# The turning steps of a chunked recurrence: products with the unit matrix in place of a mix of transpositions and products

## The reference

```
def step(state, inp):
    r_t, w_t, k_t, v_t, a_t, b_t = inp
    sa = jnp.einsum('bhvk,bhk->bhv', state, a_t)
    state = state * w_t[:, :, None, :] + sa[..., None] * b_t[:, :, None, :] \
            + v_t[..., None] * k_t[:, :, None, :]
    return state, jnp.einsum('bhvk,bhk->bhv', state, r_t)
s0 = jnp.zeros((B, H, N, N), jnp.float32)
_, ys = lax.scan(step, s0, xs)
```

## Time and profile before

| | |
|---|---|
| median of 3 runs | 2541.79 us (2538.91 to 2542.49) |
| the profiled execution | 2542.76 us, its span 2541.0 us |
| TensorE busy | 2371.4 us, 93% |
| GpSimd, VectorE, ScalarE busy | 1217.3, 1062.3 and 680.2 us |
| mean granted clock of TensorE | 0.961 |
| rchunks | from 1090.29 to 1311.8 us |

### The profile page before, as it was taken

One profiled execution on the slowest core, in us unless ns is written; L12 is line 12 of the kernel. 1 busy time (PEld: TensorE's weight loads), 2 busy tenths in 40 slices (PEclk: granted clock), 3 DMA queues, 4 the chain that ended last, 5 costly groups with the idle time before them and its releaser, 6 DMA issues.

```text
span 2541.0 us, 39706 instructions
## 1 busy us (share of the span) xinstructions
PE 2371.4 (93%) x15724; PEld 1730.5 (68%) x15724; DVE 1062.3 (42%) x1674; ACT 680.2 (27%) x1255; POOL 1217.3 (48%) x690
## 2 busy tenths in 40 slices
PE   4999998899999799989989967998999999899999
PEld 1445776688878444479966645666887787688877
DVE  5975852555500346643341344663224431422200
ACT  2125112333300234423323113672002231333300
POOL 1007885588876000000025401557877325688876
PEclk8999999999999799989989985998999999999999
DMA  7630532222222112200002140001323231232222
GB/s 278 233 105 26 220 128 67 66 99 99 91 91 97 44 62 70 66 13 4 4 11 73 60 157 1 2 2 58 100 92 107 88 103 58 75 99 95 95 91 99
DMA packets 59336, 211.63 MB, mean 83 GB/s; under 512 B 6720, under 2 KB 7752, under 8 KB 59200
## 3 DMA queue, kind: packets, MB, share of 16 engines
q1 hardware_dynamic: 48816, 175.61, 20.6%
q0 software_dynamic: 6432, 22.45, 2.5%
q10 hardware_dynamic: 3952, 11.58, 1.2%
HBM read 207.45 MB, written 8.45 MB: 85 GB/s over the span
## 4 chain that ended last, share of the span: by engine, by line
PE 64%; POOL 18%; issue 11%; DVE 4%; ACT 1%; DMA 1%; POOLq 0%; ACTq 0%; DVEq 0%; SPq 0%
PE banks L368 14%; POOL WH L404 9%; PE banks L424 9%; PE banks L425 9%; PE banks L426 9%; POOL WL_A L407 8%; PE banks L1473 3%; PE banks L1428 2%; PE banks L561 2%; PE banks L574 2%; PE banks L593 2%; DMA W<-stream 1%; PE banks L1508 1%; PE banks L1506 1%; PE banks L1926 1%
## 5 line engine op out<-in xcount | busy, mean ns | idle before, releaser
L404 POOL TENSOR_TENSOR WH<-W,ZERO 128x1024 fp32r<-128x1024 f32 x240 | 467.4, 1947 | 681.9 <-PE banks L426 371.5
L407 POOL TENSOR_TENSOR WL_A<-W,WH 128x1024 fp32r<-128x1024 f32 x164 | 419.9, 2560 | 12.9
L368 PE MATMUL banks<-H,W 128*128 128x512 f32 x752 | 332.7, 602 | 20.1 <-ACT H L735 15.1
L424 PE MATMUL banks<-HF,WH 128*128 128x512 f32 x704 | 276.6, 393 | 14.7 <-DVE HF L516 7.7
L368 PEld LDWEIGHTS banks<-H,W 128*128 128x128 f32 x752 | 144.3, 193 | 207.2 <-issue 204.1
L425 PE MATMUL banks<-HF,WH 128*128 128x512 f32 x704 | 275.7, 392 | 0.0
L426 PE MATMUL banks<-HF,WL_A 128*128 128x512 f32 x704 | 275.4, 391 | 0.0
L425 PE MATMUL banks<-HR,WH 128*128 128x512 f32 x416 | 168.3, 404 | 0.0
L424 PEld LDWEIGHTS banks<-HF,WH 128*128 128x128 f32 x704 | 132.9, 189 | 47.3 <-issue 15.7
L426 PEld LDWEIGHTS banks<-HF,WL_A 128*128 128x128 f32 x704 | 133.3, 189 | 27.7
L425 PEld LDWEIGHTS banks<-HF,WH 128*128 128x128 f32 x704 | 133.3, 189 | 26.9
(11 more groups left out here) (414 smaller groups left out, 4591.6 us busy)
## 6 DMA issues: line engine op xcount, KB each, us to landing
W<-stream SPq DMA_DIRECT2D x328, 512.0 KB, 3.5
BIG<-stream ACTq DMA_DIRECT2D x20, 512.0 KB, 6.3
BIG<-stream POOLq DMA_DIRECT2D x12, 512.0 KB, 6.8
bias_rows<-bias_lines POOLq DMA_DIRECT2D x1, 4096.0 KB, 21.9
BIG<-bias_rows POOLq DMA_DIRECT2D x1, 4096.0 KB, 16.9
X<-x_t POOLq DMA_DIRECT2D x1, 2048.0 KB, 16.4
bias_rows<-bias_lines POOLq DMA_DIRECT2D x1, 2048.0 KB, 18.8
BIG<-bias_rows POOLq DMA_DIRECT2D x1, 2048.0 KB, 11.0
```

Source lines behind the costliest of these rows:

```text
L368: last = nc.tensor.matmul(bank, W[:, slot, (lo + k) * P:(lo + k + 1) * P], r, start=(k == 0), stop=(k == len(rhs) - 1))
L404: nc.gpsimd.tensor_tensor(WH[:, half, :], W[:, slot, :], ZERO[:, 0:1].to_broadcast([P, D]), ALU.add)\
L407: nc.gpsimd.tensor_tensor(WL[stage][half], W[:, slot, :], WH[:, half, :], ALU.subtract)\
L424: nc.tensor.matmul(out_ap, w_hi, hi, start=start, stop=False)
```

## The change

In turned, the instructions whose result goes to the partitions 0 to 63 (to == 0) were transpositions, and those whose result goes to 64 to 127 were products of the tile with the unit matrix. Of the 16 instructions of a step 8 were of each kind, in the order T P P T in each group of four. Now all 16 are products with the unit matrix. Operands, targets, order of the heads and counters stay.

```diff
--- before.py
+++ after.py
@@ -1502,10 +1502,7 @@
                             at = two_banks(BANK[n])(j)[to:to + CHUNK, :]
                             tile = src[lo:lo + DH, j, c * CHUNK:(c + 1) * CHUNK]
                             eye = CON[lo:lo + DH, K0["ident"] + lo:K0["ident"] + lo + DH]
-                            if to == 0:
-                                last = nc.tensor.transpose(at, tile, eye)
-                            else:
-                                last = nc.tensor.matmul(at, tile, eye, start=True, stop=True)
+                            last = nc.tensor.matmul(at, tile, eye, start=True, stop=True)
                 last.then_inc(c_pe, 1)
 
             def apart(c, n):
```

## The result

| | before | after |
|---|---|---|
| median, six runs each | 2539.61 us | 2521.83 us (2515.2 to 2527.41) |
| ratio | | 0.993, 95% interval 0.9911 to 0.995 |
| again, with the experiments beside it | 2538.06 us | 2523.33 us, ratio 0.9946 (0.993 to 0.9962) |

What follows compares the result with a forecast made beforehand. TensorE was taken to bound the edited stage, by 2.6 over the next engine. From 2542.76 us, 33.1 + 1.0 - 0.5 - 3.5 = 30.1 saved gave 2512 after a median correction; forecast 2509 to 2516, range with rivals 2505 to 2521.

Steps and rivals of the forecast that it cites:

- layout argument: Turning step: its products use all four row-half and column-half combinations, so 0.49 us for 32 records, not the squares' 0.95.
- floor of 25 ns a record: Skill page's start-to-start minimum: 32 records would want 0.80 us, time some 2517; refused because the trace shows 14.7 ns.
- Instruction supply: -3.5: Denser fast stretches around turning steps lose about 0.7 us a chunk instead of 0.29, some 3.5 us over 8 chunks.
- 33.1 + 1.0 - 0.5: Saved us: 23 full-clock turning steps 33.1, first low-clock step 1.0; less 0.5 for ScalarE copies exposed in chunk 0.
- Rival 2: Whole stage: instruction supply is the next bound, 8.7 us lost instead of 3.5, time 2518; chance 15%.
- Rival 4: Sequencer delivers no faster than today's mean, 31.7 ns a record; 192 more records cost 6.1 us, 2549; chance 2%.
- Rivals 1 and 5: First: turning step costs 0.95 us, 2520, 9%. Second: unseen ScalarE and VectorE chain leaves nothing to 10 us, 2%.
- VectorE and ScalarE lose cover: Recurrence chunks: shorter turning steps hide less of these engines' work, but they have 15 us of idle a chunk.
- the tightest wait: Apart 11 waiting on the copy of N2: producer moves along with it, so the 0.15 us of slack stay.
- rival 3: Nothing lost in supply, and the clock rises earlier at the stage's front, up to 1.5 us; 2508; chance 18%.

## Why the prediction was wrong

- **The array's side was right.** The turning step costs 0.53 us; TensorE's busy time in a chunk fell by 4.0 us, 4.3 forecast; in the stage from 211.7 to 179.4. The layout argument (four combinations against two) and the refusal of a floor of 25 ns a record hold. No new wait on ScalarE or VectorE showed in the six chunks; in chunk 0 the two on ScalarE came to 0.31 and 0.23 us where 0.5 in all had been taken off; GpSimd's start moved with the stage, from 1312.16 to

```profile
1295.07 1.89 POOL L404 TENSOR_TENSOR WH<-W,ZERO 128x1024 fp32r<-128x1024 f32 x1 [206.08 <-DVEq L352]
```

- **The term that failed is "Instruction supply: -3.5"**, with its upper end of 8.7. I priced the gaps that the earlier trace rows showed, three in six chunks, and scaled them by how dense the stretches become. They were the visible edge of a rate. Measured: 18.5 and 23.0 us of waiting for instructions in the two profiles, against 0.5 before. The sum with that term, 33.1 + 1.0 - 0.5 - 18 to 23, gives 11 to 16 us. The fall of the granted clock at the stage's end, for which the sum has no term, takes 1.4 and 3.2 of it. The stage shows 8 to 14.5 and the time 13 to 23. That the time lay less than 1 us above the range is no sign that the sum was nearly right: the supply term was too small by 15 to 20 us. Part of that is made up outside the stage, by what looks like luck: there the clock was at the half for 189 us before and for 158 and 176 us in the two profiles after, and half of the difference, 16 and 7 us, is about what their spans gained beyond the stage (13 and 7).
- **What the rows would have told.** The earlier trace rows has a block every 4.1 us. I read it as the speed at which things went, not as a speed with a limit near it. The transfers' own records before held nothing closer than 3.36 us, though in the fastest stretches 128 records take 2.7 us by TensorE's start times (150 in 3.0). Single blocks of 2.8 to 3.0 us passed without a gap there; in each the next transfer had started by 0.5 us behind the block's first instruction, and not 1.1. A chunk of 832 records is 6.5 blocks, 24 us at 3.75: the answer was one division away, once the limit is known.
- **The rivals.** Rival 2 named the mechanism and gave it 15%, with a price of 8.7 us where 18 to 23 were lost. Rival 4 had it too strong: its price was the mean of today's rate, 31.7 ns a record; 3.75 us a block are 29.3 ns. So the truth lay between two of my cases, and its consequence, that the number of instructions counts in dense stretches, was rival 4's. Rivals 1 and 5 fell.
- **"VectorE and ScalarE lose cover" and the tightest wait** came out as forecast. The front of the stage too: T6 of chunk 0 went from 2.85 us to 0.91, 0.98 forecast:

```profile
1091.09 1.13 PE L1505 MATMUL banks<-CON,BIG 64*64 64x64 f32 x32 [0.55 <-DVE BIG L1619]
1092.00 2.17 PE L1473 MATMUL banks<-H 64*64 64x64 f32 x54
```

The granted clock rose at 1092.9 us, 5.2 us into the stage, where before it took 8.9 (just after 1099.1):

```profile
1085.00:1092.90 7.90, 4.65 (x114) 4.46 (x116) 6.13 (x10) 0.55 (x1) 1.04 (x2) 0.50 0.27 85
1093.10:1100.00 6.90, 6.11 (x181) 5.88 (x176) 1.60 (x3) 2.28 (x4) 0.00 (x0) 1.00 0.01 2
```

In all six profiles with products alone at full width it rose 5.2 to 5.4 us into the stage, in all five with transpositions in T6 8.6 to 8.9 (and some 12 in the three with squares of 32 columns). So the half of rival 3 that speaks of the clock came true: the front of the stage, up to apart 11 of chunk 1, took 5.6 and 6.2 us less than before, where the sum's own terms give 4.8. Its other half, no loss in supply, was as wrong as could be. The Trainium skill's page "TensorE: Matmul & The Clock Gate", section "Part 4: PE-mode transpose", says that a transposition doesn't count as busy for the clock; these eleven profiles agree with that and don't show why. The three with short or narrow squares rose as late with products alone as with transpositions, so the kind of the first step isn't all.

The Trainium skill's page "Runtime: NRT & Kernel Launch", section "Instruction fetch mechanics", has the fetch in blocks of 16 KB, 256 instructions, and says that crossing a block's end is mostly hidden. The first agrees with 50 and 52 blocks in the stage and with the places of the gaps; the second doesn't hold where small products run: 18.5 us of 205.5 were spent waiting for blocks.

## What to carry to other kernels

Where one engine runs hundreds of short instructions back to back, count its instructions before pricing its work: here, in dense stretches, blocks of 256 came every 3.7 to 3.9 us on average (at 3.75: 14.7 ns an instruction, 29.3 a pair of load and matmul), and a step that is cheaper for the array but longer in instructions gains only down to that line. Price it block by block: in each round one block of slow steps took 4.4 to 4.6 us, and the dense ones behind it waited all the same. An idle gap in the middle of a step that the profile puts down to "issue" is to be laid beside the starts of the instruction queue's transfers, and its place counted in instructions: gaps a multiple of 256 apart are the ends of blocks; a few of them in the kernel before mean that the limit is near, not that it costs what they sum to. Of two ways to end the alternation of kinds, prefer the one with fewer instructions: sorting the step by kind gave as much as products alone, with 384 instructions less.

## What the runs showed of the hardware

- A change between transposition and product, in either direction, keeps the neighbours from overlapping: eight of each in turn cost 1.93 us, eight and then eight at most 0.86.
- A square of 64 x 64 in two corners costs the same with 32 streamed columns as with 64 (0.90 to 0.93 us for 32 records), and 0.60 when the load too has 32 columns: for these products the weight loads set the pace.
- The granted clock rose 3.2 to 3.7 us earlier in the stage where the first turning step was products alone. It fell again at the stage's end in both profiles of the kernel after, for 3.4 and 10.2 us, and not in that of the kernel before.
- Instruction blocks: transfers of 0.9 to 1.5 us, then 1.4 us until TensorE goes on, in every kernel; no two starts closer than 3.2 us in any of the stages. 275 of 276 gaps stand at the end of a block of 256 instructions.
